# Rotation in the projection, modulation rows in the linear attention, first experts in four f32 lanes of 96 places, spare blocks tested by eights

## What is computed

```python
h_lat = modulate(rms_norm(x, norm_mix_g), sh1, sc1)        # 1024 tokens, h_ctx the same for 256 context tokens
dq, dk, dv, gq, gk, gv, gr, lrf, lrb = split(h @ w_in)
q_l = apply_axial_rope(dq_l, cos, sin); k_l = apply_axial_rope(dk_l, cos, sin)   # context keys are not rotated
a_l = diff_attend(q_l, concat(k_c, k_l), v_all, lam)       # differential attention, 4 heads
o_l = gla_chunked(forward) + flip(gla_chunked(backward))   # gated linear attention, 4 heads, chunks of 64
x = x + gt1 * (concat(a_l, g_l) @ w_out)
h2 = modulate(rms_norm(x, norm_ffn_g), sh2, sc2)           # sh2, sc2, gt1, gt2: rows of silu(c) @ w_ada + b_ada
x = x + gt2 * hier_moe(h2)     # 32 experts, hidden 512, the top 2 of the best of 4 groups per token
# second block: recurrent branch, latent attention, then 64 experts with hidden 256, top 2 of one of 8 groups
y_block = (silu(xi @ w_gate[e]) * (xi @ w_up[e])) @ w_down[e]
```

## Time and profile before

| | |
|---|---|
| time, median of 3 runs (lowest to highest) | 3530.84 us (3528.47 to 3532.21) |
| the profiled execution: its own time, its span | 3531.45 us, 3529.7 us |
| instructions | 40094 |
| PE busy | 2965.5 us (84%) |
| PE weight loads | 2114.2 us (60%) |
| DVE busy | 1744.8 us (49%) |
| ACT busy | 1280.5 us (36%) |
| POOL busy | 294.0 us (8%) |
| DMA | 702.19 MB, mean 199 GB/s |

### The profile page before, as it was taken

How to read it: one execution, slowest core, us unless ns; L and a number is a source line. 1 busy time by engine, 2 the same in 40 slices (tenths; PEclk the granted TensorE clock), 3 DMA queues, 4 the chain that set the end, 5 groups by cost and what they waited for, 6 DMA issues and landing times. The chain is left out here.

```text
span 3529.7 us, 40094 instructions
## 1 busy us (share of the span) xinstructions
PE 2965.5 (84%) x14540; PEld 2114.2 (60%) x14540; DVE 1744.8 (49%) x2646; ACT 1280.5 (36%) x1689; POOL 294.0 (8%) x416
## 2 busy tenths in 40 slices
PE   5999889967969999994799998787898896887771
PEld 3887537655757888883777786544566772333230
DVE  4111348846678889884656312355555453111112
ACT  5111135554237777773445312233333310100101
POOL 0000200001010000001000000130001101111112
PEclk7999889978979999997899999998999997999995
DMA  4322586010549999995511222200003529999985
GB/s 186 106 81 69 201 307 259 1 57 34 175 182 404 403 406 406 406 405 205 180 48 42 72 83 82 86 14 1 1 1 126 177 104 407 420 420 421 417 368 197
DMA packets 200569, 702.19 MB, mean 199 GB/s; under 512 B 27482, under 2 KB 75533, under 8 KB 150003
## 3 DMA queue, kind: packets, MB, share of 16 engines
q1 hardware_dynamic: 157668, 582.75, 42.9%
q0 software_dynamic: 23040, 67.14, 5.0%
q10 hardware_dynamic: 19728, 50.50, 3.6%
HBM read 587.93 MB, written 129.16 MB: 203 GB/s over the span
## 5 line engine op out<-in xcount | busy, mean ns | idle before, releaser
L368 DVE TENSOR_TENSOR exp_w_low<-exp_raw,exp_w_high 128x2048 fp32r<-128x2048 f32 x192 | 437.0, 2290 | 71.1 <-ACT exp_w_high L2379 71.1
L2379 ACT CAST exp_w_high<-exp_raw 128x2048 fp32r<-128x2048 f32 x192 | 366.6, 1911 | 126.6 <-PE exp_ps_y L2351 58.0
L2622 PE MATMUL exp_ps_g<-exp_gu,exp_xT 128*64 128x512 f32 x1024 | 265.4, 677 | 90.7 <-DMA exp_gu<-in_exp_w 85.0
L2622 PEld LDWEIGHTS exp_ps_g<-exp_gu,exp_xT 128*64 128x64 f32 x1024 | 88.3, 154 | 247.3 <-issue 213.9
L2325 PE MATMUL exp_ps_g<-exp_w_low,exp_xT_high 128*128 128x512 f32 x512 | 206.4, 403 | 5.8 <-DVE exp_xT_low L368 5.8
L2326 PE MATMUL exp_ps_g<-exp_w_high,exp_xT_low 128*128 128x512 f32 x512 | 203.4, 397 | 0.0
L2327 PE MATMUL exp_ps_g<-exp_w_high,exp_xT_high 128*128 128x512 f32 x512 | 203.1, 397 | 0.0
L2720 DVE TENSOR_TENSOR exp_h<-exp_sg,exp_ps_g 128x256 f32<-128x256 f32 x32 | 19.6, 612 | 340.9 <-ACT exp_sg L2676 340.9
L639 PE MATMUL inproj_ps<-inproj_w_low,h1T_high 128*128 128x512 f32 (+1 forms) x448 | 173.7, 388 | 12.9 <-DVE inproj_w_low L368 12.9
L640 PE MATMUL inproj_ps<-inproj_w_high,h1T_low 128*128 128x512 f32 (+1 forms) x448 | 173.3, 387 | 0.0
L641 PE MATMUL inproj_ps<-inproj_w_high,h1T_high 128*128 128x512 f32 (+1 forms) x448 | 173.3, 387 | 0.0
(11 more groups left out here) (543 smaller groups left out, 6670.3 us busy)
## 6 DMA issues: line engine op xcount, KB each, us to landing
exp_gu<-in_exp_w SPq DMA_DIRECT2D x64, 2048.0 KB, 28.4
exp_raw<-in_expert_w_gate SPq DMA_DIRECT2D x64, 1024.0 KB, 7.2
exp_raw<-in_expert_w_up SPq DMA_DIRECT2D x64, 1024.0 KB, 7.4
exp_raw<-in_expert_w_down SPq DMA_DIRECT2D x64, 1024.0 KB, 8.0
exp_dn<-in_exp_w SPq DMA_DIRECT2D x32, 2048.0 KB, 27.4
scratch_y<-da_zero SPq DMA_DIRECT2D x1, 32256.0 KB
dap_ada_slab<-in_w_ada SPq DMA_DIRECT2D x16, 1024.0 KB, 7.9
scratch_y<-exp_y ACTq DMA_DIRECT2D x32, 512.0 KB, 8.5
```

The costliest lines, as they stand in the source:

```text
L368: return nc.vector.tensor_tensor(low, x, high.bitcast(F32), ALU.subtract)
L2379: nc.scalar.copy(w_h[:, c], raw[:, b]).then_inc(w_high, 1)
L2622: last = nc.tensor.matmul(ps_g[side(e)], xT[:, m.par, k, side(e)], gu[:, m.buf, :, e, k, :], start=(k == 0), stop=(k == KD - 1))
```

## The change

**Projection.** `diff_prepare` is gone. The items of the first two slabs, queries and keys (18 items, `TURNED`), are not stored. ACT takes them from PSUM to the stage ring, POOL and DVE rotate the 16 that are not context, PE turns each item four items after its matmuls, and ACT places it in `da_qT` or `da_kT`, which now exist from here on. Lambda and the value load move into the attention's own block; the values are still stored and loaded again.

```diff
+    TURNED = ends[1]
+    LAG = BUF
+    rotated_items = [n for n in range(TURNED) if items[n][1] >= n_ctx]
...
+                def turn(n):
+                    if n in rotated_items:
+                        pe.wait_ge(rotated, rotated_items.index(n) + 1)
+                    else:
+                        pe.wait_ge(taken, n + 1)
+                    if n >= 2:
+                        pe.wait_ge(placed, n - 1)
+                    for h in range(DA_H):
+                        last = nc.tensor.transpose(ps_t[:, n % 2, h * P:(h + 1) * P], stage[:, n % BUF, h * P:(h + 1) * P],
+                                                   core.ident[:])
+                    last.then_inc(turned, 1)
...
                     last.then_inc(summed, 1)
+                    if n - LAG < TURNED:
+                        turn(n - LAG)
...
+            @block.gpsimd
+            def _(pool):
+                pool.wait_ge(table_in, 32)
+                for j, n in enumerate(rotated_items):
+                    pool.wait_ge(taken, n + 1)
+                    if j >= 1:
+                        pool.wait_ge(rotated, j)
+                    a, d = halves(stage[:, n % BUF]), halves(cross[:])
+                    for half in range(2):
+                        for ax in range(2):
+                            last = nc.gpsimd.tensor_tensor(
+                                d[:, ax::2, half, :], a[:, ax::2, 1 - half, :],
+                                table(n, 1)[:, ax:ax + 1, :].broadcast_to([P, S // 64, 16]), ALU.mult)
+                    last.then_inc(crossed, 1)
...
+                def rotate(j, n):
+                    dve.wait_ge(taken, n + 1)
+                    dve.wait_ge(crossed, j + 1)
```

```diff
+                    def conditions(c, half):
+                        pe.wait_ge(ada_loaded[half], 16 * (c + 1))
+                        if half == 0 and c >= 1:
+                            pe.wait_ge(sums_copied, c)
+                        for l in range(LANES):
+                            last = nc.tensor.matmul(ps_x[l * LANE:(l + 1) * LANE, :], core.cond[:, half * LANES + l],
+                                                    slab[:, half, l], start=(half == 0), stop=(half == 1))
+                        last.then_inc(ada_used, 1)
...
                     for n in range(STEPS):
+                        if 0 <= n - 3 < PARTS:
+                            take_row(n - 3)
+                        if 0 <= n - 2 < PARTS:
+                            take_sums(n - 2)
                         if n < KT:
                             gate(n)
```

```diff
+LANE_BLOCKS = 3
+LANE_EXPERTS = 4
+class LaneWeights:
+    RAW, PARTS = 18, 6
...
+                for i in range(weights.RAW, len(weights.order)):
+                    e, c = weights.order[i - weights.RAW]
+                    sp.wait_ge(gu_done if c in weights.GU else y_done, weights.last_block[e] + 1)
+                    weights.load(sp, i)
...
+                    for c in weights.GU:
+                        of_lane = weights_in(n, c)
                         half, z = c // 2, c % 2
                         for j in range(HK):
                             k = half * HK + j
+                            for l, lane in enumerate(lanes):
+                                last = nc.tensor.matmul(ps_g[lane, z], xT[:, n % 2, k, lane], raw[:, of_lane[l], j * F:(j + 1) * F],
+                                                        start=(k == 0), stop=(k == KD - 1))
```

**Spare blocks.** Their number is rounded up to a multiple of eight, 24 and 32, and each engine tests once per eight:

```diff
-                with eng.Fori(0, rt.over) as j:
-                    with eng.If(j < used):
-                        body(j)
+                with eng.Fori(0, rt.over // BEYOND_EACH) as group:
+                    with eng.If(group * BEYOND_EACH < used):
+                        with eng.Fori(0, BEYOND_EACH) as m:
+                            body(group * BEYOND_EACH + m)
```

841 lines of the change are left out of this document (371 added, 470 removed).

## The result

The changed kernel takes 3438.43 us (median of four runs, 3433.18 to 3442.17) against 3531.24 us for the kernel before in the same session: a ratio of 0.9737, 95% interval 0.9721 to 0.9754. The forecast was 3368, range 3335 to 3430: the sign and those of all six terms are right, the size is 70 us off, just outside the range. The profiled execution took 3439.67 us, span 3437.8, so the change from the profiled 3531.45 is -91.8 where the sum said -163. Of all executions only one, of e15_again, fell in a slower state (3970.01 us at a mean clock of 0.725), and it is left out.

The account below looks back on a forecast made before the run. Each stage between barriers has its own limit: PE in the projection, transfers in the second experts. From 3531.45 us, -85 + 10 + 2 + 15 - 79 - 26 = -163 gave 3368 us, range 3335 to 3430.

Parts of the forecast that it names:

- terms 1, 3, 6: The separate rotation block goes, -85; lambda's small work moves into the attention, +2; spare blocks asked by eights, -26.
- term 5: First experts, first load to next block's first load: 24 blocks instead of 32, limited by transfers, -79 us.
- a group is 0.44 us, so a block at full clock is 7.09 + 3.63: First experts: PE time of four f32 lane matmuls; with transposes a block takes 12.3 us.
- PE needs 56% of the time, and the transfers set the end: First experts: 218.1 MB at 415 GB/s take 526 us, 21.9 us a block, longer than PE's work.
- the sign that the prediction named for being wrong: First experts: the forecast is wrong if PE does not wait for loads there; no size given.
- (a): Clock stays low in the first experts, a block takes 24.6 us and the gain of 86 is gone: 3459 us, 7%.
- (d): First experts: lanes of 32 columns run two at a time, not four; 22.9 us a block, 3395 us, 4%.
- (b): The rotation's chain on Pool and DVE binds the projection: +29 us, 3397 us, 10%.
- (c): One expert has more than 96 assignments, so eight spare block bodies run, 312 us: 3680 us, 2%.
- term 4: Modulation rows move into the linear attention's first block: 1.9 us a step, +15 us.
- they fit: Linear attention: weights of 2 MB a step, 5 us at 415 GB/s, asked for a step ahead, cost nothing.
- 2: Projection takes the transposes: 18 items with 4 each on PE, +10 us; the rest of the rotation costs 0.

Follow-up runs that it names:

- e15_again: Changed kernel with a third buffer for the halves of w_ada, bias loads and row stores in Pool's queue, run again: 3430.93 us.
- e1: Changed kernel with the first experts multiplying only half of the features, all loads, waits, copies and stores kept: 3397.13 us.
- e11: Changed kernel with only the first two halves of w_ada loaded in the linear attention, the 14 later loads left out: 3427.99 us.
- b1: Kernel before with h1T at the high end of SBUF and the opening's tiles on the left: 3539.03 us.
- e13: Changed kernel with a third buffer for the halves of w_ada, and bias loads and row stores in Pool's queue: 3429.31 us.
- e14: As e13, with PE's order in the linear attention changed to chunk_states first and sum_row last: 3431.94 us.

## Why the prediction was right or wrong

**Right: terms 1, 3, 6.** The rotation's block went whole, -85.0. Lambda cost 1.7 of the 2 priced. The tests gave 26.6 of 26; that nothing behind them would take longer was wrong by some 6 us.

**Wrong: term 5, and the step is "a group is 0.44 us, so a block at full clock is 7.09 + 3.63".** I divided the 7.09 us of the earlier trace rows by 16 pairs of lanes because the row says x32. But the code behind that row issues 16 matmuls, 8 pairs: the record count is twice the instruction count for an f32 product. A pair is 0.89 us there, and a group of four 0.87 here. Blocks are 22.66 us, 24 of them 544, and 37 us pass from the first load to the first product. That makes 581 of the 583 us measured from the first load to the last down product, where the forecast had 535. The 48 us between are most of the 70. "PE needs 56% of the time, and the transfers set the end" follows from the same error; PE needs 103% of it, and the sign that the prediction named for being wrong, that PE does not wait for loads in this stage, is what the profile shows. The other steps of the term held. Transfers alone would have ended the stage at 535 (e1: 535.3), and the last store through POOL cost 5.4 us of the 7. The page "FP8 and Floating Point Precision" of the Trainium skill, section "TensorE Precision Notes", gives true FP32 four passes through the array. The trace agrees nearly: 2 x 429 = 858 ns is 3.8 times the 227 ns at which split matmuls of 512 columns start one after another. Had I set that beside the row, x32 could not have been 32 matmuls, since 0.44 us is the time of two passes.

A check was at hand in the trace of before: 3 split matmuls of 233 ns each do for 128 places what an f32 group does in 858 ns for four lanes of 32. So the new form is 23% slower for each product on PE, and gains only by its 24 blocks instead of 32: 32 x 72 x 0.233 = 537 us before, 24 x 48 x 0.429 = 494 after.

**Rivals.** (a), a low clock, did not occur: 1.00 in the stage. Where PE does wait, in e1, the clock is 0.88 and the stage still keeps the transfers' pace. (d) gave 22.9 us a block, close to the 22.66 measured, by a mechanism that is false. Its 3395 is also too low by its own figures: with the start at 1051 that (a) uses, 24 blocks of 22.9 us end at 1601, 51 us later than the forecast's 1550, which is 3419. Four lanes of 32 columns do run at once, since a group of them takes 0.86 us from start to start, and a pair of 64 columns takes the same (3405.50 to 3412.39 in the earlier trace rows, 8 pairs); each takes twice as long as I thought. The check of (d) has the same misreading: the 32 records of the earlier trace rows are four groups of 1.33 us. A number that comes out near is no support for its story. (b), the rotation's chain, did not bind: PE has no wait in the projection. (c) did not occur, no spare block ran.

**Wrong in part: term 4, "they fit" for the weights and 0.44 us for each matmul.** The added work costs about 13 us (e11), near the +15 by luck, since PE's part of it was priced at half. The loads' wait was priced at nothing, and is about 11. I compared bytes with bandwidth (2 MB a step, 5 us) and said "asked for a step ahead". With one buffer for each half a load is asked for when its own place is free, hence its 6.3 us from issue to landing are hidden only in part: over the 14 reloads some 11 us of them show.

**Wrong by a term that was missing: 2.** The transposes are +7.9 (10 priced). The other 9 come with the new place of h1T (b1: +9.0), a line of the diff that I took for bookkeeping. The +5 of all other stages are for the most part the two stretches behind the tests.

## What to carry to other kernels

Before a duration from a trace is divided by its record count, count the instructions of that line in the code: in these traces an f32 matmul has two records, so a cost per matmul read off the count is half the true one. A transfer that has one buffer per piece can show part of its latency in every turn, even where its bytes need less time than the step has; a third buffer is the test, and here it brought back 4 to 8 of 11 us. When a wait chain closes on itself (ACT for PE, PE for DVE, DVE for PE), no single link of it proves the cause: take each candidate away, and let the one whose removal shortens the step speak.

## What was unexpected

A record of four f32 lanes of 32 columns starts every 429 ns, whatever the DMA engines do beside it (401 or 216 GB/s) and wherever its stationary tile lies. Split matmuls do depend on the place: 227 ns in every stage with both operands below 173 KB of a partition, 231 to 238 in the projection with one of them at the high end, 9 to 10 us in its 1344 matmuls. And a queue order that looks worse, with the chunk products between two uses of the weights, was 5 to 8 us better. The likely reason is that it spreads the requests for the loads: with a third buffer the same two orders are 1.3 us apart (e13, e14). No run tested the spacing of the requests alone.
